# Another order of the steps on every engine: RWKV-7, attention and retention with fp32 weights

## What is computed

```python
def first_block(x, ...):                     # x: (1, 1024, 1024) fp32
    p = rms_norm(x, pre_norm_w) @ w_in       # one projection for all branches and gates
    p_rwkv, p_conv, p_pool, p_gate = split(p)
    y_a = rwkv7_branch(token_shift(p_rwkv, mu_shift), ...)   # 8 heads of 64
    y_b = short_conv_branch(p_conv, conv_w)  # 3 taps, gated
    y_c = pool_branch(p_pool, pool_w, pool_scale)  # windows 2, 4, 8, 16, then a 128x128 mix each
    proj = einsum('nbsc,ncd->nbsd', stack([y_a, y_b, y_c]), w_branch)
    merged = einsum('bsnd,nbsd->bsd', sigmoid(p_gate), proj)
    return x + rms_norm(merged @ w_out, post_norm_w)

def rwkv7_branch(...):                       # the serial part
    kk = k * k_k;  kk = kk / max(sqrt(sum(kk * kk)), 1e-12)      # per head
    y = lax.scan(_rwkv7_step, ...)           # state*w + (state.a) b + v k ; y = state r
    y = (y - mean(y)) * rsqrt(var(y) + GN_EPS) * gn_w + gn_b     # group norm, per head
    return (y + sum(r * k * r_k) * v) * silu(z)

def second_block(x, ...):
    aq, ak, av, rq, rk, rv, rg = split(rms_norm_2(x, attn_norm_w) @ w_in)
    y_attn = windowed_gqa_sink(rope(norm(aq)), rope(norm(ak)), av, sink)  # 8 heads, 2 kv, |i-j| <= 128
    ret = bidirectional_retention(rope(rq), rope(rk) / 8, rv, ...)        # 8 heads, chunks of 128
    h = x + concat([y_attn, silu(rg) * rms_norm_2(ret, ret_norm_w)]) @ w_out
    m = rms_norm_2(h, ffn_norm_w)
    return h + (silu(m @ w_gate) * (m @ w_up)) @ w_down                   # D_FF 2816
```

## Time and profile before

| | before |
|---|---|
| runs, median (lowest) | 2289.69 us (2288.56) |
| the profiled execution, its own time | 2289.23 us |
| its span | 2287.4 us |
| busy PE / DVE / ACT / POOL | 2261.0 / 1390.4 / 786.4 / 526.7 us |
| granted PE clock, mean | 0.997 of full speed |
| matmul instructions | 12500 |

### The profile page before, as it was taken

One profiled execution on the slowest core, in us unless ns is written; L12 is line 12 of the kernel. 1 busy time (PEld: TensorE's weight loads), 2 busy tenths in 40 slices (PEclk: granted clock), 3 DMA queues, 4 the chain that ended last, 5 costly groups with the idle time before them and its releaser, 6 DMA issues.

```text
span 2287.4 us, 31119 instructions
## 1 busy us (share of the span) xinstructions
PE 2261.0 (99%) x12500; PEld 1861.9 (81%) x12500; DVE 1390.4 (61%) x2279; ACT 786.4 (34%) x1309; POOL 526.7 (23%) x386
## 2 busy tenths in 40 slices
PE   8999999999999999999999999999999999999999
PEld 7888788887787888888887778888888888888887
DVE  5677777768858444764458787654866666631323
ACT  5323333333334333232234355432333333242210
POOL 3212322122103221242122121200222222250300
PEclk9999999999999999999999999999999999999999
DMA  4121211221233335743132121143222222262242
GB/s 155 45 60 50 59 55 41 57 59 55 70 103 111 114 110 208 264 147 129 65 79 52 41 56 47 33 120 120 84 79 84 84 83 84 67 206 77 81 141 72
DMA packets 245951, 208.56 MB, mean 91 GB/s; under 512 B 44080, under 2 KB 217776, under 8 KB 245808
## 3 DMA queue, kind: packets, MB, share of 16 engines
q1 hardware_dynamic: 245808, 206.57, 28.9%
HBM read 152.00 MB, written 47.71 MB: 87 GB/s over the span
## 4 chain that ended last, share of the span: by engine, by line
PE 89%; DVE 6%; issue 1%; POOL 1%; ACT 1%; DMA 1%; SPq 0%; DVEq 0%; ACTq 0%
PE PS L120 86%; PE PS L123 3%; POOL sm L129 1%; DVE Yt L137 0%; DVE sm L1968 0%; SPq L146 0%; DVE Ntmp L129 0%; DVE Nn L129 0%; DMA ro<-kr 0%; DMA Wraw<-in_w_in_dram 0%; DVE Cc L1832 0%; DVE ro L129 0%; DVE ST L137 0%; DVE qx L129 0%; DVE Wlo L129 0%
## 5 line engine op out<-in xcount | busy, mean ns | idle before, releaser
L120 PE MATMUL PS<-Hhi,Whi 128*128 128x512 f32 (+1 forms) x1544 | 498.2, 391 | 4.0 <-DVE Hlo L129 2.4
L120 PE MATMUL PS<-Hlo,Whi 128*128 128x512 f32 (+1 forms) x1544 | 496.9, 390 | 0.0
L120 PE MATMUL PS<-Hhi,Wlo 128*128 128x512 f32 (+1 forms) x1544 | 496.8, 390 | 0.0
L120 PEld LDWEIGHTS PS<-Hhi,Whi 128*128 128x128 f32 x1544 | 284.6, 189 | 62.2 <-issue 6.1
L120 PEld LDWEIGHTS PS<-Hhi,Wlo 128*128 128x128 f32 x1544 | 284.8, 189 | 58.2 <-issue 5.2
L120 PEld LDWEIGHTS PS<-Hlo,Whi 128*128 128x128 f32 x1544 | 285.4, 189 | 56.5 <-issue 2.8
L126 ACT ACTIVATE Whi<-Wraw 128x512 fp32r<-128x512 f32 x218 | 135.7, 622 | 514.3 <-PE PS L120 511.0
L129 DVE TENSOR_TENSOR Wlo<-Wraw,Whi 128x512 fp32r<-128x512 f32 (+1 forms) x136 | 120.1, 883 | 166.1 <-ACT Whi L126 165.2
L129 POOL TENSOR_TENSOR Wlo<-Wraw,Whi 128x512 fp32r<-128x512 f32 x82 | 116.5, 1422 | 398.9 <-ACT Whi L126 398.7
L129 DVE TENSOR_TENSOR Ntmp<-Nn 32x30 f32<-32x30 f32 (+14 forms) x240 | 94.1, 392 | 27.2 <-DMA Nn<-scr_ns 20.7
L120 PE MATMUL PS<-YMhi,Wlo 128*128 128x512 f32 (+1 forms) x300 | 99.2, 378 | 0.0
(11 more groups left out here) (421 smaller groups left out, 4354.6 us busy)
## 6 DMA issues: line engine op xcount, KB each, us to landing
Wraw<-in_w_in_dram SPq DMA_DIRECT2D x126, 256.0 KB, 2.9
scr_g<-stg SPq DMA_DIRECT2D x24, 512.0 KB, 3.0
tg<-scr_g SPq DMA_DIRECT2D x24, 512.0 KB, 4.3
scr_fb<-fb SPq DMA_DIRECT2D x22, 512.0 KB, 4.1
fin<-scr_fb SPq DMA_DIRECT2D x22, 512.0 KB, 3.8
gwA<-in_w_in_dram SPq DMA_DIRECT2D x40, 256.0 KB, 3.4
wA<-in_w_gate_dram SPq DMA_DIRECT2D x38, 256.0 KB, 3.2
wA<-in_w_up_dram SPq DMA_DIRECT2D x38, 256.0 KB, 3.3
```

The costliest lines, as they stand in the source:

```text
L120: return self.h.matmul(out, lhsT, rhs, start=start, stop=stop, skip_group_check=True)
```

## The change

Only the strings of ORDER for all five engines and PICKS are other ones. Each stream has the same steps in the same sequence within itself, and no line of code besides changes. The first of the 12 lines for PE:

```diff
@@ ORDER = { "pe":
-        "a5d33a2d3a2d2a2d15ad2ad19a2d16a2d106pd5pd8pd20id4pd17sdsd2sdsd4id5pd4sd6pd11pd23id56pd4id5sd3sd3sd5s"
+        "a5d33a2d3a2d2a2d15ad2ad45a2d3a2d94pd6pd12pd21id5id5pd5s2d5s2d5pd6pd8spd21id46pd4id7sd6sd6sd7s2d4scd5"
```

More of the change, by code:

```diff
@@ new lines @@
+        "6sdmd2md2sd2sd2sdcd5cs2dcd5cs2d3cds2dcd5csd2cd19gd28sd6sd6sd7s2d4scd4cds2cd4cd4cd5cd5cd4cd35gd681n2d"
+        "12n2d12n2d19n2d23n2d24n2d24n2d44n2d107kv2d9k2d36kd11k2d12rd6v2d5r2d13td2rxd6yd4td3td7wtxd5xrd9kyrwrt"
+        "d2kdtyd2kd2rw2td9xd5yd6t2d10rx2d4vyvwydxdwrwrd4xd2xd2twrdxd7yd4td2td3x2d4y2d6w3td12xdkydtd2td2rxd2kd"
+        "xydkd2yrwrd3w2rtd4yd6xkd3td2tyd3xyd2xd2kdkw2d2rdtwd2xd3v2d3ytd3tdr2xd4xdyd4yd2rw3td8xd4yd2td2td11rxd"
+        "4xd5kr2dyd2yk2d2wrw2yd14yd5xdkyd3twxdxd3k2d4kyd2rdt2d5v2dw2yk2d2ydrwrd4xd2rdtd7yd2xdxd8t2dydywtd5w2d"
@@ new lines @@
+        "xd16rdtd5trwrxd5xrwd5kd13k2d111n2d11n2d11n2d11n2d21n2d24n2d24n2d36n2d1136o2d21o2d21o2d21o2d21o2d21o2"
+        "d28o2d19od9o",
+    "act":
+        "q2w2awa3q4a2wa4q2a7w2ewewep5w2epwpwes2ws2p2wfp3swpwpfw4fws2wfsws5wsfs3wpgswegp4w2epspsw2es3ws3ws4p2w"
+        "p3gswfpgwpwfwswfs2ws3ws5ws2pwfgwgwep4sws2pwes2pswswesws4gpwpfp3sgw2fpwpw3fws2wfs2fwfs4wfs4pwsgwegp3w"
+        "pspswespwswesws5wfs2p2wfgp3fgwfspwpwfw2f3w2fs2wsf2s3wfs4ws3wfgfwgwf2wswfsfsws3wfs2fw2tSgw2tgTtS3TS3t"
+        "TStTS3t3S3t2S4tS2t2StStS3tStStStStS3tStStStStS3tStStStStS3tStStStStS3tStStStStS3tStStStStS3tStStSt2b"
+        "3wbwtwt2wtw3b2w2b2w3b2wlwlbwbw6mwm2wm2wm2wm2wm2wm2wm3n3h2n2h2n2h2nh2n2h2n2h2n2h2n2h2r3w2kwkvwv2kw2kw"
+        "k2wokw2v3k2rw2ox3y2xwyz2yzwk2x3zrkxwr3crwokx2y2xwxz2yzwvyvzvky2ry2wcx3y2woxyz2yz2w2k2x3y2xyz2kzywzrc"
+        "kr3wrk2x2oz2xy2zxywzkycwvx2v2y2x2yz2rzywzcwox3y2xwz2yzwkykrkzwr4z2wk3z2oy3wckykx3zwvzxkv2z2rwy3x2wyo"
+        "xz3xzwcx2wdxy2dwxyryrckwd2kw2iwdi3wd2i3dinh2nh2nh2nh2nh2nh2nh2nh2Sw2uwTS2wTS2uSTS2uTS5u2S2uS4uSuS2uS"
+        "4uSuS2uS4uSuS2uS4uSuS2uS4uSuS2uS4uSuS2uS4uSuS2uS4uSuS2uS4uSuS2uS4uSuS2uS4uSuS2uS4uSuS2uS4uSuS2uS4uSu"
+        "S2uS4uSuS2uS4uSuS2uS4uSuSuw2uwuw2H3wuHwH2wH2wH2wuH2wH2wuHw2uw2uw2uw2uw2uw2uH3wHwH2wHw25",
@@ L2963 @@
[L2963 removed]
+    "0123010123012301230010110100101010101101001100100110101010010101010010010101011010100101010101101000"
+    "1011010100101010101100010101101010101010101011010100110010011010101010010101010010100100101110101001"
+    "0101101101010101010001010101101010100110010101011010067523401675234016752340167523401675234016752340"
+    "1671010101010101010101010102102101011010010210110011002102110021012102100201010210210120120120120120"
+    "0102010210121021020120120101002102102110201201201201201201201020102102102102101210210210021021001201"
@@ L2964 @@
+    "0210102102102102100120120120120120112102102102102020102102102011020120102011020210101021010110010210"
+    "1100215401672354016723540167235401672354016723540167235401672354016723540167235401672354016723540167"
+    "2201201201201201201011002311002311002311023"
 )
```

78 lines of the change are left out of this document (27 added, 51 removed).

## The result

The median after is 2292.64 us (22 runs), that of before 2287.45 us with as many runs; the three runs that stood there at the time of the prediction had a median of 2289.69. One of those three took 4918.91 us and another of the 22 took 7958.81, far outside of all others, so 2289.69 is the higher of two ordinary times. The ratio is 1.002, with a 95% interval of 1.0014 to 1.0027. So the new order costs about 5 us, where the prediction said 2 us less. The time lies in the range, 2278 to 2297, and within 2%, but on the other side of before, where rival B stood ("by the clock and late producers").

The account below looks back on a forecast made before the run. PE was taken as the bound, with 29.8 us in waits and clock to give. Terms -2.4 (kp), -1.4 (mix), +1.7 (clock) made -2.1 us, from 2289.7 to 2287.6, rounded 2287.5; range 2278 to 2297.

Parts of the forecast that it names:

- rival B: Slightly slower, about 2297 us: three more half-speed clock stretches (+5), a late bank (+1.9), Yt waits (+3); chance 0.22.
- kp (place 1): Recurrent branch, fourth unit and 386 us: POOL's earlier kp copy removes PE's two kp waits; -2.4 us, bounds -2.4 and +1.
- The mix (place 2): Pool mix: dense steps between cu,pw and RAV,BK remove PE's waits for cy and cu; -1.4 us, bounds -1.4 to 0.
- Passing: PE switching between dense and small steps: more passes, fewer places where small steps touch; 0 us, bounds -1 to +3.4.
- The stage steps: Steps of stage() on PE, now 6 to 7 dense steps apart instead of 3 to 5; claimed 0.
- the start: Last two token groups transposed 26 steps later, still 41 ahead of use; with FFN and end 0, bounds -1 to +1.
- The group norm: Recurrent branch: PE's Yt waits unchanged, fewer DVE rows ahead balancing PE's sooner arrival; 0 us, bounds -3.8 to +3.
- Yt keeps 3 to 5 us: Sign that the forecast is right: PE's list of waits still shows 3 to 5 us on the group norm's Yt.
- The clock: Attention and retention: one more half-speed stretch of PE after a series of small groups; +1.7 us, bounds -3.4 to +5.
- Place 4: End of retention: more Hlo rows on DVE could free the second bank late; 0 taken, bounds 0 to +1.9 us.
- Attention's waits: Attention and retention: PE's 3.1 us of waits replaced by others of the same kind; 0 us, bounds -3 to +4.
- Rival D: Slower by over 2%: SyncE's in-order queue holds weight loads behind waiting steps; chance 0.02.

Follow-up runs that it names:

- before_kp_first: Before, with POOL's copy kp moved ahead in two units, directly behind its power in the fourth and ahead of a weight split at 386 us; 2284.3 us, before 2287.7.
- after_hold_pool: After, with one wait added on POOL: behind the group norm's power it waits for DVE's last Yt row before its next weight split; 2285.7 us, before 2286.8.
- early_only: After's order up to the end of the gates' first half, before's order behind it; 2289.4 us, before 2286.8.
- late_only: Before's order in the first stage, after's order from there on; 2291.0 us, before 2286.8.
- late_again: The kernel late_only once more, unchanged; 2291.0 us, before 2287.5.
- best_mix: early_only with the added POOL wait of after_hold_pool; 2281.7 us, before 2287.7.
- after_yt_later: After, with PE's four transposes of Yt one to six dense steps later in each of the eight units, POOL unchanged; 2282.4 us, before 2287.6.
- best_yt_later: best_mix with PE's transposes of Yt one to four dense steps later in seven units; 2280.4 us, before 2287.6.

## Why the prediction was right or wrong

**The mark it was measured from.** It forecast a difference of -2.1 us from 2289.7. With 22 runs before is at 2287.45, so 2.2 us of the base were the chance of three runs; the profiled one (2289.23) had two half-clock stretches in attention and retention, where the mean of eight profiles with that late order is 0.9. From the better base the forecast would have been 2285.4, 7.3 us from the 2292.64 measured instead of 5.1; the range, moved as much, would still have held the time.

**kp (place 1), right.** -2.4 forecast; the list shows -1.8, and before_kp_first, which does this alone, gained 3.4 us (interval 0.9 to 5.0). **The mix (place 2), right.** Both waits are gone; RAV,BK has none, where it had 0.87 us:

```profile
567.05 1.88 PE L120 MATMUL PS<-cu,pw 128*128 128x512 f32 x4
...
572.56 1.16 PE L120 MATMUL PS<-RAV,BK 64*128 64x128 f32 x16
```

**Passing, about right.** PE's busy time less 1.7 us for each stretch between 100 and 2200 us is 2261.0 - 3.4 = 2257.6 us before and 2262.8 - 6.8 = 2256.0 after, so -1.6, against a forecast of 0 and just outside its bounds of -1 and +3.4. **The stage steps and the start, right:** no new wait of theirs stands in the list.

**The group norm, the step that failed.** "The two moves are about equal: 0; bounds -3.8 (all of it gone) to +3": it measured +5.1, outside the bounds, and a half-clock stretch of 1.7 us came behind the longest wait. The term of the sum that was mis-sized is the chain, added up from rows one by one to "8 with the releases". From the end of the last chain step to the end of the last Yt row it measured 10.0 us in the second unit, for which the sum was made, and 9.3 to 16.9 in the eight (before, 7.9 to 17.0); PE's distance, "about 8.3", was 8.8. Of the 2 us missing in the second unit, 1.1 are the last row beside POOL's split, and 1.0 the reductions, which began 1.27 us behind the chain step, where 0.25 was the time in five units before. Fewer rows ahead on DVE, counted as a gain, are what made the two rows meet; without the meeting (after_hold_pool) the waits are back at 3.9 us, and the term would have been the 0 of the forecast. That two such rows block each other is what the Trainium skill says in "SBUF — State Buffer", section "Who interferes with whom", and the price stood in a row of the trace before (the last Yt row of the sixth unit took 1.78 us); the sum used neither. Of its own signs, "Yt keeps 3 to 5 us" is the one that failed.

**The clock, right in kind.** "One more stretch: +1.7", and two to four between 1170 and 1512 us: there were three, and over all profiles 1.5 more than before. "A series of small groups" is not the cause as stated: at the second key norm the stretches came with a wait of 0.3 us ahead of the norm and went when one dense step was moved, and at step 2350 parting the steps did nothing. The rule of the Trainium skill that was set against it ("TensorE: Matmul & The Clock Gate", Part 1: idleness takes the clock down) is borne out in part. Of the ten waits of PE over 2 us behind the start, in all profiles, seven had a fall of the clock in them or right behind: four of 2.6 us (the first on Yt), and those of 4.09, 4.75 and 4.92. Waits of 2.31, 2.62 and 2.65 us had none. And of the 27 stretches in attention and retention 15 began with no wait of PE close before, the others with one of 0.1 to 1.1 us, so such waits alone don't decide it.

**Place 4, wrong in its mechanism, right in size by luck.** 0 was taken, with a bound of +1.9 us: there is 1.1 us of wait, but on an Hlo row, not on the bank, and by a late load, which the prediction did not follow to its release.

**Attention's waits, about right.** Apart from the clock, the two late orders are equal: with 1.7 us taken off for each stretch, the profiles lie at 363.3 to 364.6 us for that of before and at 363.0 to 364.4 for that of after.

**The sum.** +5.1 for Yt, -1.8 for kp, -1.4 for the mix and +1.7 for the clock give +3.6 for the first stage, where +2.9 was measured, 0.9 of it in the start, and early_only cost 2.6. In the rest the clock gives +2.6, the stages between and behind +0.4 and -0.7, and so 2.3; by the times of late_only and late_again it is 4.3 and 3.4 (intervals from 1.6 to 6.4), and by best_mix and after_hold_pool, each against its own before, 4.9. The remainder of 1 to 3 us is hardly more than the intervals, and its cause is open. Rival B was the case, with 0.22, by two of its three parts. Rival D, SP's queue, came up only in after_yt_later and best_yt_later.

## What to carry to other kernels

When an order is changed so that a row waits for nothing but its input, look at what else that same signal releases: two rows of engines that exclude each other in memory can then meet each time (here in six units of eight, before in one), and the row that a neighbour used to hold off at no cost becomes the late one. A short idle in the queue of the engine that has time gave back 6.9 us here, more than the new order had lost; but first read what else stands in that queue. And with differences of a few microseconds in 2300, one profile is one throw of the dice: the base needs as many runs as the answer.

## What the runs showed of the hardware

A two-input row of DVE (128x512) took 0.69 us alone and 1.6 to 1.8 us when POOL's split of 1.26 us had begun just ahead of it; a row with one input from PSUM was not held up. The other way round a split of 1.3 us on POOL took 8.31 us (8.24 in another kernel) beside a series of DVE's. The clock fell to 0.50 for 3.4, 6.8 or, once at the start, 10.2 us: at seven of ten waits of over 2 us, and, in attention and retention, always 1.0 to 3.6 us behind the start of a key norm's group of 16 matmuls, 15 of the 27 with no wait of PE close before. The same kernel had two such stretches in one execution of this stage and four in another.
